# x read from memory in both layouts, and the opening loads put in another order

## The reference, cut to what matters

```
h = rmsnorm(x, g[0])                 # per token: x / sqrt(mean(x^2) + eps), then times the gain g[0] per feature
p = h @ w_in                         # 1024 x 5120: hq, hf, hi, hgate, rq, rk, rv, rgate
f = lb + (1 - lb) * sigmoid(hf)      # forget gate of the scan; lb from softmax over hg_lower_bound
o_hg = scan(silu(hq), 1 - f, log(f), hi)
```

## Time and profile before

| | |
|---|---|
| three runs | 895.21, 895.42, 895.71 us |
| span of the profiled execution | 893.5 us |
| the median less the span | 1.9 us |
| TensorE busy | 884.4 us, 99% of the span |
| VectorE, ScalarE busy | 652.2 us (73%), 498.4 us (56%) |
| chain that ended last | TensorE 91%, VectorE 5%, ScalarE 2%, DMA 1% |
| mean granted TensorE clock | 0.999 |

### The profile page before, as it was taken

The page is one execution under the profiler, slowest core; times in us unless marked ns, Lnnn a source line. Parts: engine busy times, 40 slices in busy tenths (PEclk is TensorE's granted clock), DMA queues, the critical chain, the costliest instruction groups (busy, mean ns, idle before and its releaser), DMA issues.

```text
span 893.5 us, 13339 instructions
## 1 busy us (share of the span) xinstructions
PE 884.4 (99%) x5610; PEld 756.6 (85%) x5610; DVE 652.2 (73%) x790; ACT 498.4 (56%) x676; POOL 31.1 (3%) x25
## 2 busy tenths in 40 slices
PE   8999999999999999999999999999999999999997
PEld 7889888888888888888888888888879998888885
DVE  6999656569777767699567977777668895556655
ACT  6875556465444454766566544445558774366624
POOL 0000000000000000000000000000000083000000
PEclk9999999999999999999999999999999999999999
DMA  9644444466666664544336666666336344324431
GB/s 357 275 146 179 149 142 142 142 247 222 241 227 240 230 241 167 202 157 161 120 142 255 228 240 230 239 239 235 142 132 244 120 142 143 116 101 155 137 129 47
DMA packets 24155, 165.40 MB, mean 185 GB/s; under 512 B 2688, under 2 KB 2944, under 8 KB 4896
## 3 DMA queue, kind: packets, MB, share of 16 engines
q1 hardware_dynamic: 22608, 159.73, 48.9%
q0 software_dynamic: 1056, 4.34, 1.3%
q10 hardware_dynamic: 432, 0.49, 0.2%
HBM read 163.50 MB, written 1.05 MB: 184 GB/s over the span
## 4 chain that ended last, share of the span: by engine, by line
PE 91%; DVE 5%; ACT 2%; DMA 1%; issue 1%; DVEq 0%; SPq 0%; ACTq 0%
PE acc L633 30%; PE lin L594 11%; PE lin L615 6%; PE lin L622 6%; PE lin L599 6%; PE lin L616 6%; PE lin L573 3%; PE lin L581 3%; PE lin L574 3%; DVE w_lo L1889 2%; PE acc L841 1%; PE acc L725 1%; PE acc L726 1%; DVE arena L2342 1%; PE acc L735 1%; PE lin L678 1%
## 5 line engine op out<-in xcount | busy, mean ns | idle before, releaser
L1889 DVE TENSOR_TENSOR w_lo<-raw,w_hi 128x2048 fp32r<-128x2048 f32 x137 | 318.4, 2336 | 127.7 <-ACT w_hi L1384 127.1
L1384 ACT CAST w_hi<-raw 128x2048 fp32r<-128x2048 f32 x137 | 259.6, 1907 | 138.0 <-DMA raw<-in_weights 86.0
L633 PE MATMUL acc<-w_hi,f_hi 128*128 128x512 f32 x288 | 113.1, 393 | 0.0
L633 PE MATMUL acc<-w_hi,f_lo 128*128 128x512 f32 x288 | 112.4, 390 | 0.0
L615 PE MATMUL lin<-w_hi,h_both 128*128 128x512 f32 x272 | 109.4, 402 | 0.2
L594 PE MATMUL lin<-h_both,w_hi 128*128 128x512 f32 x448 | 106.7, 390 | 0.0
L616 PE MATMUL lin<-w_hi,h_both 128*128 128x512 f32 x272 | 106.3, 391 | 0.0
L594 PEld LDWEIGHTS lin<-h_both,w_hi 128*128 128x128 f32 x448 | 83.2, 188 | 16.7
L633 PE MATMUL acc<-w_lo,f_hi 128*128 128x512 f32 x288 | 78.9, 389 | 0.0
L622 PE MATMUL lin<-w_lo,h_both 128*128 128x512 f32 x272 | 68.1, 390 | 0.2 <-DVE w_lo L1889 0.2
L573 PE MATMUL lin<-h_both,w_hi 128*128 128x256 f32 x272 | 67.3, 287 | 0.0
(11 more groups left out here) (372 smaller groups left out, 1225.7 us busy)
## 6 DMA issues: line engine op xcount, KB each, us to landing
raw<-in_weights SPq DMA_DIRECT2D x149, 1024.0 KB, 4.8
rowbuf<-in_rows POOLq DMA_DIRECT2D x6, 512.0 KB, 4.0
x<-in_x_in SPq DMA_DIRECT2D x2, 512.0 KB, 4.5
raw<-in_weights SPq DMA_DIRECT2D x2, 512.0 KB, 7.3
arena<-in_const_even POOLq DMA_DIRECT2D x1, 1024.0 KB, 11.6
out<-x SPq DMA_DIRECT2D x3, 256.0 KB, 2.1
cst<-in_const SPq DMA_DIRECT2D x1, 580.0 KB, 10.4
out<-x ACTq DMA_DIRECT2D x1, 256.0 KB, 2.1
```

What stands on the lines that cost most here:

```text
L633: return pe.matmul(acc[:, at:at + 512], part_of(2 * j + k)[i][:, t * P:(t + 1) * P], w[:, k * 1024 + c * 512:k * 1024 + (c + 1) * 512], st ...
L1384: act.copy(w_hi[:, o % SPLIT, :], raw[:, j % RAW, :]).then_inc(hi_done, 1)
L1889: dve.tensor_tensor(w_lo[:, j % RAW, :], r, hi.bitcast(F32), ALU.subtract).then_inc(tile_split, 1)
```

## The change

x is handed over in two layouts: as before, and as `x_turned_in`, 128 partitions x 2048 floats, with feature k*128+p of token t at partition p, column k*256+t. The rearrangement is made on the host while the inputs are laid out. SyncE's queue then has: first half of the turned x, first half of w0, second half of the turned x, second half of w0, w1, x in the old layout, the identity, the columns 8 and up of the small column table, w2, the general constants, w3, and on as before. ScalarE's queue loads only the first eight columns, which are the gain. The halves of w1 are rounded as those of w0 are: the first by VectorE, the second by ScalarE. All the turns by TensorE in the opening are gone; the dummy matmuls are 16 in one row. `first_r` comes after all of w1 instead of within its high matmuls. VectorE's five operations on the bound columns come behind `w_lo` of w1.

```
-WARM, WARM_UP = 11264, (8, 0, 6)
+WARM, WARM_UP = 11264, 16
+XT = 8704
...
         def _(sp):
-            for t in range(TT):
-                sp.dma_start(x[:, t, :], x_in[0, t * P:(t + 1) * P, :]).then_inc(x_loaded[t], 16)
-            sp.dma_start(raw[:, 0, 0:1024], weights[0][:, 0:1024]).then_inc(first_loaded, 16)
-            sp.dma_start(raw[:, 0, 1024:2048], weights[0][:, 1024:2048]).then_inc(loaded[0], 16)
+            for i in range(2):
+                s = slice(i * 1024, (i + 1) * 1024)
+                sp.dma_start(arena[:, XT + i * 1024:XT + (i + 1) * 1024], x_turned_in[:, s]).then_inc(xt_loaded[i], 16)
+                sp.dma_start(raw[:, 0, s], weights[0][:, s]).then_inc((first_loaded, loaded[0])[i], 16)
             for n in range(1, n_tiles):
                 if n == 2:
+                    for t in range(TT):
+                        sp.dma_start(x[:, t, :], x_in[0, t * P:(t + 1) * P, :]).then_inc(x_loaded[t], 16)
+                    sp.dma_start(cst[:, 0:P], const[:, 0:P]).then_inc(s_ident, 16)
+                    sp.dma_start(colbuf[:, 8:NCOL], cols[:, 8:NCOL]).then_inc(s_small, 16)
+                if n == 3:
                     sp.dma_start(cst[:, P:C_W], const[:, P:C_W]).then_inc(s_const, 16)
...
-            for t in range(TT):
-                for _ in range(WARM_UP[t]):
-                    pe.matmul(lin[1][:, 0:512], warm[:, 0:P], warm, start=True, stop=True)
-                pe.wait_ge(s_ident, 16)
-                pe.wait_ge(x_loaded[t], 16)
-                for k in range(DC):
-                    mm = pe.transpose(acc[:, k * T + t * P:k * T + (t + 1) * P], x[:, t, k * P:(k + 1) * P], ident)
...
-            for _ in range(WARM_UP[2]):
+            for _ in range(WARM_UP):
                 pe.matmul(lin[1][:, 0:512], warm[:, 0:P], warm, start=True, stop=True)
...
             def first_r():
+                pe.wait_ge(s_ident, 16)
                 after(x_r, 2)
...
             first_projection("hf")
-            project_feature_major("hf", (1,), first_r)
+            pe.wait_ge(second_hi, 1)
+            project_feature_major("hf", (1,))
+            first_r()
             project_feature_major("hq")
...
-            act.dma_start(cst[:, 0:P], const[:, 0:P]).then_inc(s_ident, 16)
-            act.dma_start(colbuf[:, :], cols).then_inc(s_small, 16)
+            act.dma_start(colbuf[:, 0:8], cols[:, 0:8]).then_inc(gain_loaded, 16)
...
-                    ins = act.activation(h_hi[:, k, :], acc[:, k * T:(k + 1) * T], ACT.Identity, scale=col("n0g", k), bias=0.0)
+                    ins = act.activation(h_hi[:, k, :], arena[:, XT + k * T:XT + (k + 1) * T], ACT.Identity, scale=col("n0g", k), bias=0.0)
...
-            act.wait_ge(s_small, 16)
-            first_high(range(8))
-            act.wait_ge(loaded[0], 16)
-            act.copy(w_hi[:, 0, 1024:2048], raw[:, 0, 1024:2048]).then_inc(hi_done, 1)
-            split_next[0] = 1
-            split_until(2)
+            act.wait_ge(gain_loaded, 16)
+            for i in range(2):
+                act.wait_ge(xt_loaded[i], 16)
+                first_high(range(4 * i, 4 * i + 4))
+            for n in range(2):
+                act.wait_ge(loaded[n], 16)
+                act.copy(w_hi[:, n, 1024:2048], raw[:, n, 1024:2048]).then_inc(hi_done, 1)
+            split_next[0] = 2
...
             first_h_low(range(4, 8))
             dve.wait_ge(hi_done, 1)
             first_low(1).then_inc(tile_split, 1)
+            dve.wait_ge(loaded[1], 16)
+            dve.tensor_copy(w_hi[:, 1, 0:1024], raw[:, 1, 0:1024]).then_inc(second_hi, 1)
+            dve.wait_ge(second_hi, 1)
             split_next[0] = 1
             split_until(2)
+            dve.wait_ge(s_small, 16)
...
```

More of the change, by code:

```diff
@@ L229, with build @@
 GATE_ACC = dict(z=1536, sum=1568, m=1584, row=1664)
-WARM, WARM_UP = 11264, (8, 0, 6)
+WARM, WARM_UP = 11264, 16
+XT = 8704
 CROSS = 12288
 SUMS = ["ev_out", "down0_7", "od_out", "down1_7", "out"]
-def build(nc, weights, cols, rows, const, const_even, masks, x_in, out, stop=None):
+def build(nc, weights, cols, rows, const, const_even, masks, x_in, x_turned_in, out, stop=None):
     with ExitStack() as ctx:
@@ L319, in build @@
         first_loaded = sem("first_loaded")
+        xt_loaded = [sem(f"xt_loaded{i}") for i in range(2)]
+        gain_loaded = sem("gain_loaded")
+        second_hi = sem("second_hi")
         first_hi = sem("first_hi")
         first_lo = sem("first_lo")
-        x_turned = sem("x_turned")
         x_r = sem("x_r")
@@ L878, in _ @@
             pe.wait_ge(warm_ready, 1)
-            for t in range(TT):
-                for _ in range(WARM_UP[t]):
-                    pe.matmul(lin[1][:, 0:512], warm[:, 0:P], warm, start=True, stop=True)
-                pe.wait_ge(s_ident, 16)
-                pe.wait_ge(x_loaded[t], 16)
-                for k in range(DC):
-                    mm = pe.transpose(acc[:, k * T + t * P:k * T + (t + 1) * P], x[:, t, k * P:(k + 1) * P], ident)
-                    if t == 1 and k % 2 == 1:
-                        mm.then_inc(x_turned, 1)
-            for _ in range(WARM_UP[2]):
+            for _ in range(WARM_UP):
                 pe.matmul(lin[1][:, 0:512], warm[:, 0:P], warm, start=True, stop=True)
@@ L1555, in first_high @@
                 for k in ks:
-                    if k % 2 == 0:
-                        after(x_turned)
-                    ins = act.activation(h_hi[:, k, :], acc[:, k * T:(k + 1) * T], ACT.Identity, scale=col("n0g", k), bias=0.0)
+                    ins = act.activation(h_hi[:, k, :], arena[:, XT + k * T:XT + (k + 1) * T], ACT.Identity, scale=col("n0g", k), bias=0.0)
                     if k % 2 == 1:
                         ins.then_inc(ht_hi, 1)
-            act.wait_ge(s_small, 16)
-            first_high(range(8))
-            act.wait_ge(loaded[0], 16)
-            act.copy(w_hi[:, 0, 1024:2048], raw[:, 0, 1024:2048]).then_inc(hi_done, 1)
-            split_next[0] = 1
-            split_until(2)
+            act.wait_ge(gain_loaded, 16)
[6 more added lines that the diff above has]
+            split_next[0] = 2
             for t in range(TT):
@@ L2047, in first_h_low @@
                         after(ht_hi)
-                    ins = dve.scalar_tensor_tensor(h_lo[:, k, :], acc[:, k * T:(k + 1) * T], col("n0g", k), h_hi[:, k, :].bitcast(F32),
-                                                   ALU.mult, ALU.subtract)
+                    ins = dve.scalar_tensor_tensor(h_lo[:, k, :], arena[:, XT + k * T:XT + (k + 1) * T], col("n0g", k),
+                                                   h_hi[:, k, :].bitcast(F32), ALU.mult, ALU.subtract)
                     if k % 2 == 1:
@@ L2054, in _ @@
             link(dve.memset(ev("sco", 512), 0.0))
[L2055 to L2061, removed]
             first_h_low(range(2))
@@ L2070, in _ @@
             first_low(1).then_inc(tile_split, 1)
+            dve.wait_ge(loaded[1], 16)
+            dve.tensor_copy(w_hi[:, 1, 0:1024], raw[:, 1, 0:1024]).then_inc(second_hi, 1)
+            dve.wait_ge(second_hi, 1)
             split_next[0] = 1
             split_until(2)
+            dve.wait_ge(s_small, 16)
+            hl = col("hlb", 0, 12).rearrange("p (r h) -> p r h", r=3)
+            link(dve.tensor_tensor(stat[:, 84:88], hl[:, 0, :], hl[:, 1, :], ALU.max))
+            link(dve.tensor_tensor(stat[:, 84:88], stat[:, 84:88], hl[:, 2, :], ALU.max))
+            for r in range(3):
+                ins = dve.tensor_tensor(stat[:, 60 + 4 * r:64 + 4 * r], hl[:, r, :], stat[:, 84:88], ALU.subtract)
+            ins.then_inc(diff_ready, 1)
             for t in range(TT):
@@ L2685, in _host_layout @@
             "const": np.concatenate(list(_C.values()), 1), "const_even": np.concatenate(list(_CE.values()), 1),
-            "masks": level_masks(), "x_in": np.asarray(i["x"])}
+            "masks": level_masks(), "x_in": np.asarray(i["x"]),
+            "x_turned_in": np.ascontiguousarray(np.asarray(i["x"])[0].reshape(T, DC, P).transpose(2, 1, 0)).reshape(P, DC * T)}
 def kernel(**inputs):
```

## The result

The changed kernel takes 898.98 us in the median of five runs (897.64 to 899.82), the kernel before 895.45 in the five runs beside it: ratio 1.0037, 95% interval 1.0026 to 1.0049. One of those five runs took 1092.86 us, against 895.21 to 895.71 us for the others, and is left out of the ratio. The changed kernel is slower by 3.3 us by this ratio (3.5 us by the medians), where +1.4 us was forecast. The five runs form two groups: 897.64 and 897.69, and 898.98, 899.10 and 899.82 us. The profiled execution is the one of 899.10 us, with a span of 897.3 us, 3.8 us longer than before.

What follows compares the result with a forecast made beforehand. TensorE was taken as the bound. Its 2.05 us earlier start shrank to 1.05 us within w0, the loop made w3 1.14 us late and w4's low part 1.35 us: +1.4 us, 896.8 us, range 895.3 to 898.9.

Steps and rivals of the forecast that it cites:

- rival C: At w2 or w3: late landing becomes the bound, 0.9 us on top, +2.3 us in all, 897.7 us; chance 22%.
- rival D: Before w3: TensorE's clock falls in the new 2.2 us wait, 1.9 us lost, +3.3 us, 898.7 us; chance 10%.
- The forecast's own sum: Likeliest outcome: the delay reaching `w_lo` of w4 stays to the end, +1.4 us, 896.8 us; chance 45%.
- What bounds, and the direction: TensorE, busy 99% of 893.5 us, bounds; an earlier start helps only if nothing else becomes late; +1.4 us expected.
- The marks named for the trace: Signs: first matmul at 7.3 us, waits of about 1 us in w0 and 2 us at w3, w1 ending near 19.9.
- The loop behind `first_r`: From w1's end to w3: turn, copy, `w_lo` of w2, sigmoid, `w_hi` take 8.22 us; TensorE waits 2.2 us.
- The transfers up to w1: Opening loads: second half of x lands at 7.5 us, second half of w0 at 8.8, w1 at 11.3, each +-0.4.
- between these ends I take 1.0 us: Opening loads: moving identity and columns behind w1 saves 1.0 us, taken between 0.64 and 1.3 us.
- the gap of 1.3 us: Opening loads: the longest the small transfers can have cost, 3.9 us less two 512 KB transfers at 1.3 us.
- X: The end of w1 on TensorE, forecast at 19.85 us; break even needs 18.7 us or less.
- On to w4: Behind w3: `w_lo` of w3 comes 1.53 us later, 0.18 us is slack, so `w_lo` of w4 moves 1.35 us.
- The transfers behind w1: Later loads: w2 lands at 18.3 us, w3 at 26.1 us, when ScalarE wants it at 26.13; no slack left.

Runs made afterwards that it cites:

- a1: The kernel before with only `first_r` moved behind all of w1: 898.96 us, ratio 1.0038.
- d1: The changed kernel with the identity and the columns from 8 up loaded again at the start from ScalarE's queue: 899.76 us, ratio 1.0046.
- b3: The changed kernel with both halves of the turned x ahead of both halves of w0: 899.07 us, ratio 1.0035.
- c2: The changed kernel with turned x first, several loads later, w2's parts ahead of squares and factors, `Z0` ahead of the lower bound: 894.99 us, ratio 0.9997.
- a2: The changed kernel with `first_r` back within the high matmuls of w1: 898.30 us, ratio 1.0035.
- a3: The changed kernel with GpSimd's three loads waiting for w3 instead of w1: 899.03 us, ratio 1.0038.
- b1: The changed kernel with 9 dummy matmuls between w2 and w3, in TensorE's wait: 898.19 us, ratio 1.0030.
- a4: The changed kernel with `first_r` back within w1 and GpSimd's loads behind w3: 897.56 us, ratio 1.0027.

## Why the prediction was right or wrong

**The number.** The median of 898.98 us lies at the upper edge of the range (895.3 to 898.9), which reached so high only to take in the rivals C and D. The forecast's own sum, +1.4 us, was 1.9 us too low, and that the range holds the result is not its merit: it is D's price, to which the prediction gave 10%.

**What bounds, and the direction: right.** TensorE was the bound, its start came earlier by 1.8 us (2.05 forecast), and the end came later. The marks named for the trace were there: the first matmul at 7.57 us (7.3), a wait of 1.4 us within w0 (1.0), one of 2.1 us at w3 released by `w_hi` (2.2), and the sigmoid in front of it; only the end of w1 came 0.9 us later than named (20.8 against 19.9).

**The loop behind `first_r`: right.** From the end of w1 to w3 8.22 us were forecast; 8.24 us were measured here and in a1. a1 shows it alone.

**The transfers up to w1: wrong by 0.8 us.** The failed step is "between these ends I take 1.0 us". The small transfers cost 0.5 to 0.8 us (d1). The rest of the gap of 1.3 us from which the 1.0 was taken lies in a slow stretch of the DMA: from 6 to 8 us the engines moved 276 GB/s in the kernel before, with 1.3% of them on the small transfers' queue, and the changed kernel has such a stretch with these transfers gone from the opening (234 GB/s from 5 to 6 us). And with turned x and w0 taking turns in the queue the 512 KB halves came slower: the second half of w0 landed at 9.6 us, in d1 with all bytes of before ahead of it at 10.3 against 9.8 us. With x first and w0 behind it (b3 and c2) it landed at 9.1 to 9.2 us, against 9.5 to 9.8 us in all eight profiles in which they take turns. The second half of x landed at 8.43 instead of 7.5 us and held up ScalarE. So TensorE resumed at 11.13 instead of 10.2, X was 20.8 instead of 19.85, and w3 started at 29.06 instead of 28.07 us. This is 1.0 us of what the forecast lacked; the clock is the rest.

**On to w4: right in kind, too large.** 0.2 us beyond the delay of w3 were forecast. In a1, with the clock up, the low part of w4 begins at 38.68 us, +2.3 us for +2.2 us at w3, so about 0.1 us more. In the changed kernel's own profile VectorE's chain had no part in it: it waited 1.38 us for the end of w3, which the clock had made late.

**The transfers behind w1: right that they come near the bound.** w3 was forecast to land at 26.1 us, just as ScalarE wanted it. It landed at 26.7 us, while ScalarE came for it at 27.12 us, and a2 and a3 show the two causes to lie within 0.2 us of each other. In b1 and b3, with `first_r` still behind w1, ScalarE waited for the landing (27.3 and 26.9 us), so rival C's mechanism is real as well.

**The clock: the rival D came true in more than half of the runs.** It was given 10% with +3.3 us. The mechanism was right and its price near (1.9 us forecast, 1.6 measured), the chance was far too low. The argument for 10% was that shorter waits had left the clock up; the longest of them was 1.2 us, and no row could speak for 2.2. The Trainium skill (TensorE: Matmul & The Clock Gate, section "HAM oscillation — how this bites in real kernels") describes a kernel in which waits between bursts of matmuls bring the clock down to half. The traces of the changed kernel, a2, a3 and d1 show such falls, with waits of 1.7 and 2.1 us. The waits in the section's example are longer than these, so the section alone did not make the sum D's, as the prediction has it.

With the measured sizes in the forecast's own sum, w3 starts 1.1 + 1.0 us later and 0.1 us come on to w4: +2.2 us with the clock up. The two runs of the changed kernel with the clock up are 2.2 us above 895.45. The median of five lies in the other group because three of them had the clock down.

## What to carry to other kernels

An operation that another engine's list waits for is not moved to where its own engine would be idle, but to where the list behind it still makes its due time: measure the loop from it back to its engine, and compare that with the work beside it. Ask of each wait that a change makes on TensorE whether it comes near 2 us, as the waits here did; if it may, price it with the clock as well, and consider filling it. Where two causes bind at the same place, undoing one shows nothing; undo both, and look whether the edit itself made a third. And follow a lead or a delay to the end of the span: a wait of 0.33 us at 176 us took half of what the best version here had won at the start.

## What the runs showed of the hardware that was not expected

- TensorE's clock fell to the 1.2 GHz level after single waits of 1.7 us (d1) and 2.1 us (changed kernel, a2, a3), for about 3.4 us in each of the four profiles, and in 17 of 29 runs by their times. It did not in the profiled executions of a1 (2.13 us) and b3 (2.48 us before w3 and 2.51 us before w0), nor in d1 before w3 (2.12 us) or in a4 before the low part of w4 (1.78 us), and none of a4's nine runs is above 898.1 us. Waits of 1.5 us and less were never followed by a fall in a profile.
- The opening's DMA is slow for a time that depends on the order: 276 GB/s from 6 to 8 us in the kernel before and 234 GB/s from 5 to 6 us in the changed one, beside some 420 GB/s from 8 us on in both. The engines are busy meanwhile (shares of 1.03 and 0.88), so it is their packets that take longer. Why was not found, and in one order it moves: b1, with the changed kernel's opening, is slowest from 4 to 5 us (242 GB/s).

```profile
6.00:8.00 2.00, 1.58 (x13) 1.23 (x13) 0.81 (x6) 1.05 (x3) 0.00 (x0) 1.00 1.03 276
```

```profile
5.00:6.00 1.00, 1.00 (x4) 0.42 (x3) 0.00 (x0) 0.99 (x3) 0.00 (x0) 1.00 0.88 234
```
